# Reordering the blocks of an MLP and per-layer-embedding stage, on eight cores

## The reference, cut to what matters

```python
    merged = g_f * fourier_out + g_a * attn_out
    x = x + rmsnorm(merged @ w_out, norm_mix_post)

    h2 = rmsnorm(x, norm_mlp_pre)
    u = jnp.square(jax.nn.relu(h2 @ w_up))
    x = x + rmsnorm(u @ w_down, norm_mlp_post)

    e = (p @ w_ple) * jax.nn.sigmoid(x @ w_ple_gate)
    x = x + rmsnorm(e, norm_ple_post)
    return x
```

## Time and profile before

| what | us |
|---|---|
| median of the six runs | 14285.66 (13678.84 to 15070.22) |
| the two lowest runs | 13678.84, 13721.78 |
| the profiled execution | 13690.31 |
| its span on the slowest core | 13688.7 |
| spans of the eight cores | 13641.8 to 13688.7 |

### The profile page before, as it was taken

The page is one execution under the profiler, slowest core; times in us unless marked ns, Lnnn a source line. Parts: engine busy times, 40 slices in busy tenths (PEclk is TensorE's granted clock), DMA queues, the critical chain, the costliest instruction groups (busy, mean ns, idle before and its releaser), DMA issues.

```text
span 13688.7 us, 209149 instructions; the slowest of 8 cores (13641.8 to 13688.7 us)
## 1 busy us (share of the span) xinstructions
PE 11125.3 (81%) x78072; PEld 6011.1 (44%) x78688; DVE 3140.7 (23%) x5159; ACT 5386.4 (39%) x6666; POOL 2545.6 (19%) x3307
## 2 busy tenths in 40 slices
PE   3489978997899789968868999999777777777777
PEld 1146434643464356434433566666333333333333
DVE  2123332333233323334410111110311111111111
ACT  0047314731473147321110799999222222222221
POOL 1101120112011201122210000000033333333333
PEclk8799989998999899989989999999988888988888
DMA  6742133113311331133357332332322222222221
GB/s 159 187 121 50 59 125 119 50 54 129 120 50 56 132 117 51 65 137 102 109 182 250 89 80 75 80 80 68 110 86 91 93 79 77 77 91 93 90 75 67
DMA packets 748224, 1342.87 MB, mean 98 GB/s; under 512 B 372064, under 2 KB 464480, under 8 KB 710368
## 3 DMA queue, kind: packets, MB, share of 16 engines
q1 hardware_dynamic: 683088, 1104.42, 24.9%
q0 software_dynamic: 64144, 225.03, 5.8%
HBM read 1144.79 MB, written 224.92 MB: 100 GB/s over the span
## 4 chain that ended last, share of the span: by engine, by line
PE 61%; ACT 16%; DMA 9%; issue 5%; DVE 4%; POOL 3%; SPq 1%; ACTq 0%; DVEq 0%; POOLq 0%
ACT arena L736 14%; PE ps L1005 8%; PE ps L1022 8%; PE ps L752 8%; PE ps L830 5%; PE ps L642 5%; PE ps L561 3%; PE ps L528 3%; PE ps L531 3%; PE ps L1064 2%; PE ps L895 2%; PE ps L701 2%; PE ps L897 2%; PE ps L704 2%; PE ps L899 2%
## 5 line engine op out<-in xcount | busy, mean ns | idle before, releaser
L736 ACT ACTIVATE arena<-ps 128x1024 bf16<-128x1024 f32 x4096 | 3820.0, 1067 | 795.7 <-PE ps L832 791.3
L752 PE MATMUL ps<-arena 128*128 128x130 bf16 x32768 | 2556.9, 222 | 49.3 <-ACT arena L736 49.0
L752 PEld LDWEIGHTS ps<-arena 128*128 128x128 bf16 x32768 | 1872.1, 98 | 942.7 <-issue 934.1
L830 PE MATMUL ps<-arena 64*128 64x512 bf16 x4096 | 1529.5, 380 | 191.7 <-ACT arena L736 179.1
L832 PE MATMUL ps<-arena 64*128 64x512 bf16 x4096 | 1560.8, 387 | 0.0
L417 ACT ACTIVATE arena<-ps 128x512 bf16<-128x512 f32 (+2 forms) x376 | 249.2, 669 | 3211.9 <-PE ps L561 1425.3
L1005 PE MATMUL ps<-arena 128*128 128x512 bf16 x5001 | 1147.5, 391 | 75.0 <-DVE arena L424 69.7
L458 PE MATMUL ps<-arena 128*128 128x128 bf16 x2432 | 266.0, 307 | 1137.6 <-DVE arena L444 850.2
L642 PE MATMUL ps<-arena 128*128 128x512 bf16 x4011 | 949.3, 396 | 265.0 <-DMA arena<-dftp 139.7
L1022 PE MATMUL ps<-arena 128*128 128x512 bf16 x5020 | 1115.9, 382 | 49.5 <-POOL arena L1013 44.2
L788 POOL TENSOR_TENSOR arena<-arena 128x512 f32<-128x512 f32 x160 | 202.6, 1266 | 3882.2 <-DVE arena L785 3882.2
(11 more groups left out here) (111 smaller groups left out, 11871.1 us busy)
## 6 DMA issues: line engine op xcount, KB each, us to landing
arena<-b_wup SPq DMA_DIRECT2D x160, 1024.0 KB, 4.8
arena<-g_scr SPq DMA_DIRECT2D x128, 1024.0 KB, 6.4
arena<-xc SPq DMA_DIRECT2D x48, 2048.0 KB, 9.6
arena<-kt_scr SPq DMA_DIRECT2D x160, 512.0 KB, 3.9
arena<-v_scr SPq DMA_DIRECT2D x160, 512.0 KB, 4.6
arena<-dftp SPq DMA_DIRECT2D x128, 512.0 KB, 7.7
arena<-ropec SPq DMA_DIRECT2D x512, 128.0 KB, 2.2
arena<-dfts SPq DMA_DIRECT2D x128, 512.0 KB, 7.5
```

Of the source, the lines that this page charges most:

```text
L736: P.op("act", lambda e, pt=pt, b0=b0: e.activation(out=pt.rearrange("p a b -> p (a b)"), in_=ps[:, b0 * 512:b0 * 512 + 1024], func=AF.Exp, ...
L752: r = e.matmul(ps[:, bk * 512 + off: bk * 512 + off + 130], lhsT=pt[:, c, qs * 128:(qs + 1) * 128], rhs=vt[:, kc, :], start=st_, stop=Fals ...
L830: e.matmul(bank(b0), lhsT=kt[0:64, kc * 128:(kc + 1) * 128], rhs=qTh[0:64, qb * 512:(qb + 1) * 512], start=True, stop=True)
```

## The change

The body of the loop is cut into functions (m_load, m_prenorm, m_T, m_up, m_down, m_ple), and these are called in another order: the next block's load and pre-norm are issued ahead of this block's down product, its transposes and up product behind it, and then comes this block's PLE. Besides:

- w_ple is loaded once, into wple_r, ahead of the loop.
- The ring W8 has two buffers instead of three.
- The transposes for PLE go tile by tile: cast to a single buffer stg, eight transposes, one copy to x2T, which has a buffer of the bookkeeping for each tile. h2T serves the up product alone.
- tmp1 is gone; tg takes its part, so one buffer holds the tanh, the product and the scaled result of a tile.
- The square behind the relu and both residual adds move from POOL to DVE.
- The stores of x1_scr and y move from POOL's queue to ACT's.

```diff
-            P.dma("pool", lambda e, xt=xt, r0=r0: e.dma_start(out=x1_scr[r0:r0 + 512, :].rearrange("(t p) d -> p t d", p=128), in_=xt),
+            P.dma("act", lambda e, xt=xt, r0=r0: e.dma_start(out=x1_scr[r0:r0 + 512, :].rearrange("(t p) d -> p t d", p=128), in_=xt),
...
-    W8 = Ring(P, A, "w8m", 3, [128, 4096], BF16)
+    W8 = Ring(P, A, "w8m", 2, [128, 4096], BF16)
...
+    x2T = A.alloc([128, 8, 512], BF16)
+    Bx2T = [P.buf("x2T%d" % t) for t in range(4)]
...
-    tmp1 = A.alloc([128, 1024], F32)
-    Btmp1 = P.buf("tmp1m")
+    stg = [A.alloc([128, 1024], BF16) for _ in range(1)]
+    Bstg = [P.buf("stg%d" % i) for i in range(1)]
...
+    ADD_ENG = cfg.get("m_add_eng", "dve")
...
+    def m_load(bi_):
+        u, qb = blocks[bi_]
+        r0 = u * NQ + qb * 512
+        xt, Bx, _ = XR.next()
+        P.dma("sp", lambda e, xt=xt, r0=r0: e.dma_start(
+            out=xt, in_=x1_scr[r0:r0 + 512, :].rearrange("(t p) d -> p t d", p=128)), 1, Bx,
+            reads=[units[u]["Bx1"][qb]], writes=[Bx])
+        return xt, Bx
...
+    def m_up():
...
+                P.op("act", lambda e, r_=r_, bi=bi: e.activation(out=r_, in_=bank(bi), func=AF.Relu), reads=[PB[bi]], writes=[Br_])
+                P.op("dve", lambda e, r_=r_, fc=fc: e.scalar_tensor_tensor(out=uT[:, fc, :], in0=r_, scalar=1.0, in1=r_,
+                                                                           op0=ALU.mult, op1=ALU.mult),
+                     reads=[Br_], writes=[BuT[fg]])
...
+    def m_ple(bi_, xt, Bx):
...
+        for t in range(4):
+            sg, Bsg = stg[0], Bstg[0]
+            P.op("dve", lambda e, t=t, sg=sg: e.tensor_copy(out=sg, in_=xt[:, t, :]), reads=[Bx], writes=[Bsg])
+            bi = nextbank((0, 1, 2, 3))
+            bv = bank_bf(bi)
+
+            def tr(e, sg=sg, bv=bv):
+                r = None
+                for kc in range(8):
+                    r = e.transpose(out=bv[:, kc * 128:(kc + 1) * 128], in_=sg[:, kc * 128:(kc + 1) * 128], identity=ident)
+                return r
+            P.op("pe", tr, reads=[Bsg, Bid], writes=[PB[bi]])
+            copy_op(evac_eng(), x2T[:, :, t * 128:(t + 1) * 128], bv.rearrange("p (a b) -> p a b", a=8), [PB[bi]], [Bx2T[t]])
...
+        wpgt = [wload(W8, "wpg", i) for i in range(2)]
...
+            P.op("act", lambda e, yg=yg: e.activation(out=tg, in_=yg, func=AF.Tanh, scale=0.5),
+                 reads=[PB[bg_], PB[bg_ + 1]], writes=[Btg])
...
+            P.op("dve", lambda e, st=st: e.scalar_tensor_tensor(out=tg, in0=tg, scalar=st[:, 2:3], in1=gpost[:, 2, :],
+                                                                op0=ALU.mult, op1=ALU.mult),
+                 reads=[Bst, Bconst], writes=[Btg])
+            P.op(ADD_ENG, lambda e, xt=xt, t=t: e.tensor_tensor(out=xt[:, t, :], in0=xt[:, t, :], in1=tg, op=ALU.add),
+                 reads=[Btg, Bx], writes=[Bx])
+        P.dma("act", lambda e, xt=xt, u=u, qb=qb: e.dma_start(
+            out=dr["y%d" % u][qb * 512:(qb + 1) * 512, :].rearrange("(t p) d -> p t d", p=128), in_=xt),
+            1, Bx, reads=[Bx])
+
+    wple_r = A.alloc([128, 2, 1024], BF16)
+    Bwple = P.buf("wple_r", dma=True)
+    P.dma("sp", lambda e: e.dma_start(out=wple_r.rearrange("p a b -> p (a b)"), in_=wb["wple"][0].rearrange("p a b -> p (a b)")),
+          1, Bwple, reads=[Bw["wple"]], writes=[Bwple])
+    nblk = len(blocks)
+    cur = m_load(0)
+    m_prenorm(cur[0], cur[1])
+    m_T()
+    m_up()
+    for bi_ in range(nblk):
+        nxt = None
+        if bi_ + 1 < nblk:
+            nxt = m_load(bi_ + 1)
+            m_prenorm(nxt[0], nxt[1])
+        m_down(cur[0], cur[1])
+        if nxt is not None:
+            m_T()
+            m_up()
+        m_ple(bi_, *cur)
+        cur = nxt
```

More of the change, by code:

```diff
@@ L981, in build @@
     Btg = P.buf("tg")
[L982 to L1037, removed]
@@ new lines, in build, with m_prenorm @@
+    mst = {"rli": 0}
+    blocks = [(u, qb) for u in range(NU) for qb in range(NQ // 512)]
+    ADD_ENG = cfg.get("m_add_eng", "dve")
[7 more added lines that the diff above has]
+        return xt, Bx
+    def m_prenorm(xt, Bx):
+        for t in range(4):
+            st, Bst = stat4()
+            P.op("act", lambda e, t=t, st=st: e.activation(out=junk, in_=xt[:, t, :], func=AF.Square,
+                                                           scale=1.0 / 32.0, accum_out=st[:, 0:1]),
+                 reads=[Bx], writes=[Bjunk, Bst])
+            rstd_ops(st, Bst)
+            P.op("dve", lambda e, t=t, st=st: e.tensor_scalar(out=xn4[:, t, :], in0=xt[:, t, :], scalar1=st[:, 2:3],
+                                                              scalar2=None, op0=ALU.mult),
+                 reads=[Bx, Bst], writes=[Bxn4[t]])
@@ L1038, in build, with m_T, tr @@
+    def m_T():
+        for kp in range(4):
             bi = nextbank((0, 1, 2, 3))
             bv = bank_bf(bi)
-            def tr(e, bv=bv):
+            def tr(e, kp=kp, bv=bv):
                 r = None
-                for c in range(2):
+                for kk in range(2):
+                    kc = kp * 2 + kk
                     for t in range(4):
-                        r = e.transpose(out=bv[:, c * 512 + t * 128: c * 512 + (t + 1) * 128],
-                                        in_=pbf[:, t, c * 128:(c + 1) * 128], identity=ident)
-                return r
@@ L1048, in build @@
[L1048 to L1056, removed]
-                    r = None
[L1058 to L1065, removed]
-                    return r
[L1067 to L1082, removed]
@@ new lines, in m_down, with mm @@
+    def m_down(xt, Bx):
+        for t in range(4):
+            b0 = nextbank((4, 6))
+            def mm(e, t=t, b0=b0):
+                r = None
+                for half in range(2):
+                    for fc in range(32):
+                        r = e.matmul(bank(b0 + half), lhsT=uT[:, fc, t * 128:(t + 1) * 128],
+                                     rhs=wdn[:, fc, half * 512:(half + 1) * 512], start=(fc == 0), stop=(fc == 31))
+                return r
+            P.op("pe", mm, reads=list(BuT) + [Bwdn], writes=[PB[b0], PB[b0 + 1]])
+            y = ps[:, b0 * 512: b0 * 512 + 1024]
+            st, Bst = stat4()
+            P.op("act", lambda e, y=y, st=st: e.activation(out=junk, in_=y, func=AF.Square, scale=1.0 / 32.0,
+                                                           accum_out=st[:, 0:1]), reads=[PB[b0], PB[b0 + 1]], writes=[Bjunk, Bst])
+            rstd_ops(st, Bst)
+            P.op("dve", lambda e, y=y, st=st: e.scalar_tensor_tensor(out=tg, in0=y, scalar=st[:, 2:3], in1=gpost[:, 1, :],
+                                                                     op0=ALU.mult, op1=ALU.mult),
+                 reads=[PB[b0], PB[b0 + 1], Bst, Bconst], writes=[Btg])
+            P.op(ADD_ENG, lambda e, xt=xt, t=t: e.tensor_tensor(out=xt[:, t, :], in0=xt[:, t, :], in1=tg, op=ALU.add),
+                 reads=[Btg, Bx], writes=[Bx])
```

69 lines of the change are left out of this document (66 added, 3 removed).

## The result

| what | before, us | after, us |
|---|---|---|
| median of the runs | 14415.8 (16 runs, 13678.84 to 15091.37) | 14228.88 (8 runs, 13476.91 to 14607.43) |
| lowest run | 13678.84 | 13476.91 |
| profiled execution | 13690.31 | 13495.33 |
| its span on the slowest core | 13688.7 | 13493.4 |
| stage of the change, slowest core | 3757.8 | 3548.0 |

The ratio is **0.987, 95% interval [0.981, 0.993]**: faster by 1.3%, less than the 2% that a measurement of this kernel tells apart.

A forecast was written before the change was run, and what follows sets the result against it. TensorE's idle time at phase seams and its clock were taken to bound the kernel. Block terms summed to 177.0 us against 187.7, saving 193 us in 18 blocks plus 20 at the ends: 13690 - 213 = 13477 us, range 13300 to 13640.

The forecast's parts named there:

- stop in down, the refill: Down's third tile waits 7.4 us for reads queued behind a pre-norm that needs the y store, then the x load.
- clock loss behind it: In down, the granted clock falls while PE stands idle at the third tile, costing 2.2 us per block.
- down's end to up's start: Next block's transposes start at once, but eight serial copies to h2T delay up until 10.1 us after down.
- up: Up product takes 57.1 us with its slow start, as before; squares on DVE hidden, two weight buffers cost zero.
- up's end to PLE: Cast, eight transposes and copy for four tiles, with one stg buffer, put PLE 13.5 us after up's end.
- PLE: PLE takes 29.9 us plus up to 0.6 for each of three tiles from the tg hold: 31 us.
- last block: The last block has no next one in it: 55.4 + 17.5 + 31 = 104 us instead of 187.7.
- The chain's terms: From PLE's last matmul E: residual add E+8.5, store E+16.3, load E+26.2, squares E+31.3, down's first-tile reads done E+35.1.
- The way to the second copy: After down, DVE's second h2T copy waits for the last tile's square, POOL, multiply and add: 5.1 us.
- eats the gain: Rival: store and load 12 us longer bring the block back to 187.7 and the time to 13690; chance 0.17.
- Covered: Rival: x load lands by E+18, down runs through, 9.6 x 18 = 173 us saved: 13304; chance 0.20.
- Starved: Rival: two weight buffers make up wait for weights; at 11.7 us landing, 600 us more: 14080; chance 0.08.

The follow-up runs named there:

- the kernel with the copies first: Changed kernel with the next block's transposes and h2T copies issued ahead of the last down tile's reads; period 172.4 or 173.6 us, one run 14361.7.
- the first two experiments: Each against the changed kernel: pre-norm issued behind down's second tile, period 167.2 us; y store and x load cut into four one-tile transfers, period 168.3.
- the dense kernel: Changed kernel with pre-norm and transposes moved into down, PLE's transposes inside up, alternating banks, more buffers; period 132.8 us, median 13699.07 and, repeated, 13455.12.
- the run of 12655: One execution, 12655 us, of the repeated changed kernel with pre-norm and transposes inside down, PLE's transposes inside up, alternating banks; PE busy 98% over 2400 us.

## Why the prediction was right and wrong

**The step that failed is the level.** I wrote "my number is for runs at that level", the level of the profiled execution, 13690, and took the 213 us off it. The time of a kernel here is the median of all its runs, and this was 14286 in the six runs that I had and 14228.88 for after. The range, 13300 to 13640, was laid around the wrong base and does not contain it. In its place the runs show a median of 14228.88 over eight executions, of which three took 13477 to 13569, inside the range, and five 14202 to 14607; of the sixteen of before, three took 13679 to 13722 and thirteen 14084 to 15091. The saving of 213 us on the median of 14286 would have been 14073, or, as the ratio 13477/13690 = 0.984, 14063; both still 1% under 14228.88. On 14415.8, the median of before with the later runs in it, 0.984 gives 14192, within 0.3%. So with the right base most of the rest of the miss is, as far as these numbers tell, the scatter of a median of six runs, which the spread of 13679 to 15070 announced; the range should have allowed for it. That 13477 is equal to the lowest run is luck: the middle of the three is 13507.

**The sum held at its own level.** The stage on the slowest core (0 before, 7 after) fell by 3757.8 - 3548.0 = 209.8 us, against 213 predicted. It began there 14.5 us later (9945.42 against 9930.90; by cores it goes both ways, core 0 began 49 us earlier and core 7 by 23 later), and 14.5 + 3.2 is the 18 us between 13477 and 13495. That the change lies within 2% follows from the sum: 1.6% by it, 1.3% measured.

| term per block, us | predicted | after, core 7 |
|---|---|---|
| stop in down, the refill | 7.4 | 6.2 |
| clock loss behind it | 2.2 | 2.6 |
| down's end to up's start | 10.1 | 10.1 |
| up | 57.1 | 58.3 |
| up's end to PLE | 13.5 | 14.1 |
| PLE | 31 | 31.0 |
| period | 177.0 | 177.5 |
| last block | 104 | 104.1 |

The 55.4 of down and 0.2 are in the period beside the rows shown. The term that was too low is up, by 1.2 us: I took it from an up behind 3.2 us of idle time, and here it stands behind 8.2. In the kernel with the copies first, behind 4.4 us, it took 56.8 and 57.9. The stop was put 1.2 us too high, and the two cancel; that the period came out within half a us is in part this luck.

**Slips in the working.** The chain's terms as written add to E + 34.6 (8.5 + 7.7 + 9.8 + 4.96 + 2.4 + 1.28), not E + 35.1, so the stop by them is 6.9 instead of 7.4, and the total 9 us lower; the measured stop is 6.2. The way to the second copy is 4.9 us by its four terms, not 5.1 (the trace has 5.1). In the rival that eats the gain, 12 us more a block do bring the time back to 13690, but the block to 189; 10.7 bring the block to 187.7.

**The refill** came as written: adds end at E + 9.0 (8.5 predicted), the store lands 6.6 after its issue (7.3), the load 7.9 (9.4), reads end at E + 33.3 (35.1). The transfers were faster than in before's rows, the add half a us later. The Trainium skill (DMA: Bandwidth & Descriptors, section Anatomy of one DMA) gives its fit, an estimate of 6.8 us for 2 MB, for transfers that GpSimd issues. POOL's stores come near it, 7.1 us at the least. The store on ACT, 6.6, and the load on SP, 7.9, are on other queues, for which the section gives no fit, and my use of it for the load went beyond what it states; the stop of 4.3 by it and my 7.4 lie on either side of the measured 6.2. That the stop is the refill, and that the place of the pre-norm in the lists is what lets it reach down, the first two experiments show.

**The rivals.** "Covered" did not come about, but its price was right: with the stop removed the period was 167.2 and 168.3, where 177.0 - 9.6 = 167.4 had been worked out. "Eats the gain" fell, the chain being shorter than mine. "Starved" fell: PE's waits on core 7 have no row for b_wup, though one landing took 13.1 us (median 4.9); on three other cores there is one single wait for it, of 0.2 to 0.8 us.

**What was put at nothing.** The square behind the relu on DVE was hidden (up has no wait inside it). I did not try the w_ple load and the store of x1_scr each by itself; with both stores moved back the period changed by 0.5 us, and no wait of PE in the stage names w_ple in before or after. That the engine changes alone are worth 4.3 us a block in the old order I had not seen; I costed them only in the new one.

## What to carry to other kernels

When the next block's work waits for a load and is issued early on engines that work through their lists in order, place it behind the reads that free the present product's PSUM, not ahead of them: here that place alone was worth 10 us of 177. A load whose buffer is freed by the store of the block just ended begins only when that store has landed, whatever its place in the code; follow the chain from the last write of the old block. Work out the period of a block by terms, and state beside it whether the base is the profiled execution or the median that will be measured.

## What the runs showed of the hardware

- A 2 MB store issued by ACT landed in 6.6 us at the least, by POOL in 7.1. The medians of the cores are mostly at these values and reach 7.9 (ACT, core 2 of the dense kernel) and 8.5 (POOL, core 1 of before). The issue took 0.38 us on ACT and 0.84 to 0.86 on POOL. A 2 MB load on SP took 7.9 in the median behind ACT's store, 9.4 in before.
- 32 transposes took 1.95 us directly behind a running down product and 3.5 to 3.6 behind 9 to 17 us of idle time, at the end of which the granted clock stands at 0.50.
- With eight cores in the dense stage the granted clock of the profiled core averaged 1.00 over 2400 us, in the run of 12655.
